# Order of VectorE's work in the attention of the second block, and where the heads' norm weight is multiplied in

## The reference, cut to what matters

```python
ya = sparse_attention(aq, ak, av, iq, ik, iw, k_sel)      # 8 heads of 64, keys chosen by an index (top 128)
yb = diff_attention(bq, bk, bv, lam)                      # 4 heads, two softmaxes each, values of 128
#   p = softmax(q k / 8, causal);  attn = p[:, :, 0] - lam * p[:, :, 1];  yb = attn @ v
yb = (rms_norm(yb, b_subln) * (1.0 - lam_init))           # b_subln: one weight for each of the 128 columns of a head
g_a, g_b = split(sigmoid(gates + gate_bias))
merged = g_a * (ya @ w_up_a) + g_b * (yb @ w_up_b)
x = x + merged @ w_out
```

## Time and profile before

| | |
|---|---|
| time, median of 3 runs | 2447.8 us (2446.33 to 2454.46) |
| the profiled execution | 2451.56 us, span 2450.0 us |
| PE busy | 2279.2 us (93%) |
| DVE, ACT, POOL busy | 1266.3 us (52%), 838.8 us (34%), 363.2 us (15%) |
| mean granted clock of TensorE | 0.976 |

### The profile page before, as it was taken

The page is one execution under the profiler, slowest core; times in us unless marked ns, Lnnn a source line. Parts: engine busy times, 40 slices in busy tenths (PEclk is TensorE's granted clock), DMA queues, the critical chain, the costliest instruction groups (busy, mean ns, idle before and its releaser), DMA issues.

```text
span 2450.0 us, 28572 instructions
## 1 busy us (share of the span) xinstructions
PE 2279.2 (93%) x11029; PEld 1718.7 (70%) x11029; DVE 1266.3 (52%) x2310; ACT 838.8 (34%) x1478; POOL 363.2 (15%) x273
## 2 busy tenths in 40 slices
PE   7899988789889999899999999999989999999999
PEld 4785676455334776677778888887667778888887
DVE  4633446631113696676554434458776746443442
ACT  4334433321101445444242223244454334322221
POOL 0111123000000454331000000035433200000000
PEclk9999999889999999999999999999999999999999
DMA  8116310269998121221223222222212212333222
GB/s 294 53 53 208 110 35 10 95 235 334 359 383 289 61 80 59 61 69 52 78 86 101 97 95 95 91 78 77 78 53 69 69 43 95 97 100 96 91 90 78
DMA packets 198570, 281.61 MB, mean 115 GB/s; under 512 B 13308, under 2 KB 125732, under 8 KB 198436
## 3 DMA queue, kind: packets, MB, share of 16 engines
q1 hardware_dynamic: 197872, 278.60, 34.1%
q10 hardware_dynamic: 564, 1.18, 0.1%
HBM read 277.65 MB, written 2.10 MB: 114 GB/s over the span
## 4 chain that ended last, share of the span: by engine, by line
PE 72%; DVE 15%; DMA 5%; ACT 5%; issue 2%; SPq 1%; POOL 0%; DVEq 0%; ACTq 0%
PE PS L621 19%; PE PS L623 18%; PE PS L622 18%; PE PS L2248 3%; PE PS L1378 3%; PE PS L2288 2%; DMA RX<-in_w_up_dram 1%; DVE AL L824 1%; PE PS L2179 1%; PE PS L1360 1%; DVE AL L816 1%; DMA RAW<-in_w_up_dram 1%; DVE AL L803 1%; PE PS L2304 1%; DVE CO L800 1%
## 5 line engine op out<-in xcount | busy, mean ns | idle before, releaser
L621 PE MATMUL PS<-OPH,WHI 128*128 128x512 f32 x1224 | 503.2, 411 | 15.5 <-DVE OPL L1414 7.7
L623 PE MATMUL PS<-OPH,WLO 128*128 128x512 f32 x1224 | 486.5, 397 | 0.0
L622 PE MATMUL PS<-OPL,WHI 128*128 128x512 f32 x1224 | 482.2, 394 | 0.0
L609 POOL TENSOR_TENSOR WLO<-RAW,WHI 128x1024 fp32r<-128x1024 f32 (+1 forms) x107 | 253.0, 2370 | 1310.5 <-ACT WHI L576 1307.2
L576 ACT ACTIVATE WHI<-RAW 128x1024 fp32r<-128x1024 f32 (+2 forms) x286 | 294.1, 1032 | 445.7 <-PE PS L623 437.0
L593 DVE TENSOR_TENSOR WLO<-RAW,WHI 128x1024 fp32r<-128x1024 f32 x179 | 214.6, 1200 | 382.8 <-ACT WHI L576 382.8
L621 PEld LDWEIGHTS PS<-OPH,WHI 128*128 128x128 f32 x1224 | 233.1, 190 | 81.9 <-issue 32.0
L623 PEld LDWEIGHTS PS<-OPH,WLO 128*128 128x128 f32 x1224 | 232.7, 190 | 53.1
L622 PEld LDWEIGHTS PS<-OPL,WHI 128*128 128x128 f32 x1224 | 233.7, 191 | 46.5 <-issue 1.0
L621 PE MATMUL PS<-WHI,OPH 128*128 128x512 f32 (+2 forms) x576 | 235.3, 409 | 8.2 <-ACT AL L758 3.6
L623 PE MATMUL PS<-WHI,OPL 128*128 128x512 f32 (+2 forms) x576 | 221.3, 384 | 0.0
(11 more groups left out here) (410 smaller groups left out, 3316.0 us busy)
## 6 DMA issues: line engine op xcount, KB each, us to landing
RAW<-in_w_in_dram SPq DMA_DIRECT2D x102, 512.0 KB, 3.5
RAW<-in_w_ffn_in_dram SPq DMA_DIRECT2D x88, 512.0 KB, 3.5
RX<-in_w_gate_dram SPq DMA_DIRECT2D x42, 512.0 KB, 7.6
RX<-in_w_down_dram SPq DMA_DIRECT2D x42, 512.0 KB, 11.4
RAW<-in_w_ffn_out_dram SPq DMA_DIRECT2D x40, 512.0 KB, 3.4
RAW<-in_w_mod_dram SPq DMA_DIRECT2D x36, 512.0 KB, 4.5
RX<-in_w_up_dram SPq DMA_DIRECT2D x32, 512.0 KB, 11.3
RAW<-in_w_up_dram SPq DMA_DIRECT2D x25, 512.0 KB, 9.8
```

The lines of the kernel that those rows point to most:

```text
L609: lo_p.up(G.e.tensor_tensor(q.flo, q.flat, q.fhi.bitcast(F32), ALU.subtract), ("w", q.i))
L621: T.e.matmul(o, a[0], b[0], start=first, stop=False)
L622: T.e.matmul(o, a[0], b[1], start=False, stop=False)
L623: return T.e.matmul(o, a[1], b[0], start=False, stop=last)
```

## The change

It does six things, in both layers. (1) DVE's dense pieces of a step come ahead of its index entries, and `best_at` takes one entry in step 0 and none in steps 9 and 14 (38 in all in place of 39). (2) A row's end is done by itself, at lag 7, in place of two at lag 4. (3) The leasts of kind a are taken in pairs, at even steps. (4) From step 49 a step has one dense piece; PE does one more behind the last values, turns the last block, and does the last two then; ACT and DVE split that block ahead of what remains of their dense pieces. (5) The multiplication by `b_subln` goes: it is loaded as a column into `VT`, and becomes the scale of ACT's copy and DVE's subtraction behind the transposes; the multiplication by the reciprocal root is done for one block each in steps 21, 23, 25 and 27. (6) L3077, one element per partition, is a tensor_scalar with two scalar operands.

```diff
-                          ("gb", d["gate_bias_2"].rearrange("a (k p) -> (a k) p", p=128))))):
+                          ("gb", d["gate_bias_2"].rearrange("a (k p) -> (a k) p", p=128)),
+                          ("sub", d["b_subln_2"])))):
...
-                          ("bq", "b_q_norm_2", 64), ("bk", "b_k_norm_2", 64), ("sub", "b_subln_2", 128))] +
+                          ("bq", "b_q_norm_2", 64), ("bk", "b_k_norm_2", 64))] +
...
+            V.e.tensor_copy(VT[:, 192:194], ps(PB["vt"])[:, 192:194])
...
-        def act_block_split(name, dst):
+        def act_block_split(name, dst, gain=None):
             A.wait_ge(*turned["blk", name])
-            split_a.up(A.e.activation(dst, ps(PB["blk", name]).rearrange("p (g n) -> p g n", g=4), ACT.Copy), name)
-
-        def dve_block_split(name, low, high):
+            split_a.up(A.e.activation(dst, ps(PB["blk", name]).rearrange("p (g n) -> p g n", g=4), ACT.Copy,
+                                      scale=1.0 if gain is None else gain), name)
+
+        def dve_block_split(name, low, high, gain=None):
...
+                split_v.up(V.e.scalar_tensor_tensor(low, src, gain, high.bitcast(F32), ALU.mult, ALU.subtract), name)
...
-                at = each_third(y, 4)
-                if at and at[1] % 2:
-                    for r in (first + 4 * at[0] + at[1] - 1, first + 4 * at[0] + at[1]):
-                        dve_rope_end(r)
+                at = each_third(y, 7)
+                if at:
+                    dve_rope_end(first + 4 * at[0] + at[1])
...
-        parts_at = lambda s: 3 if s < 32 else 2
+        parts_at = lambda s: 3 if s < 32 else 2 if s < 49 else 1
...
-        best_at = lambda s: 1 if s in (1, 2, 3, 9, 14, 15) else 2 - s % 2 if 18 <= s < 32 else 2 if 32 <= s < 38 else 0
+        best_at = lambda s: 1 if s in (0, 1, 2, 3, 15) else 2 - s % 2 if 18 <= s < 32 else 2 if 32 <= s < 38 else 0
...
-                some(dense, 1)
+                some(dense, min(parts_at(s) - 1, 1))
...
+            some(dense, 1)
+            pe_block_turned(("a2", l, 7), YR2[:, 3], tidy["a2", l, 7], D)
             for _ in dense:
                 pass
-            pe_block_turned(("a2", l, 7), YR2[:, 3], tidy["a2", l, 7], D)
...
-                    for v in u.cs:
+                    for v in u.cs if u.kind == "b" else [] if u.h % 2 else units[s:s + 2]:
...
-                    t = diff_v.up(V.e.scalar_tensor_tensor(u.r, u.cs[0].rs, LAM[:, 4 * l:4 * l + 1], u.r, ALU.mult, ALU.mult))
+                    t = diff_v.up(V.e.tensor_scalar(u.r, u.cs[0].rs, LAM[:, 4 * l:4 * l + 1], u.r, ALU.mult, ALU.mult))
...
-                    if u.no in (15, 16):
-                        for i in (0, 1) if u.no == 15 else (2, 3):
-                            y = QB[:, :, 128 * i:128 * i + 128]
-                            V.wait_ge(*diff_v.up(V.e.tensor_tensor(
-                                y, y, Y16[:, i].unsqueeze(2).to_broadcast([128, 4, 128]), ALU.mult)))
-                            diff_v.up(V.e.tensor_tensor(y, y, R(f"sub{l}").unsqueeze(1).to_broadcast([128, 4, 128]),
-                                                        ALU.mult), ("y", l, i))
+                    if u.no in (16, 18, 20, 22):
+                        i = (u.no - 16) // 2
+                        y = QB[:, :, 128 * i:128 * i + 128]
+                        diff_v.up(V.e.tensor_tensor(y, y, Y16[:, i].unsqueeze(2).to_broadcast([128, 4, 128]), ALU.mult), ("y", l, i))
+                some(dense, parts_at(s))
                 some(index_, best_at(s))
-                some(dense, parts_at(s))
+            dve_block_split(("a2", l, 7), OPL[:, 0:4, sparse_tokens(7)], OPH[:, 0:4, sparse_tokens(7)])
             for _ in dense:
                 pass
-            dve_block_split(("a2", l, 7), OPL[:, 0:4, sparse_tokens(7)], OPH[:, 0:4, sparse_tokens(7)])
```

More of the change, by code:

```diff
@@ L1406, in pe_block_turned @@
             ring.give(b, (split_v, name))
-        def act_block_split(name, dst):
+        def act_block_split(name, dst, gain=None):
             A.wait_ge(*turned["blk", name])
-            split_a.up(A.e.activation(dst, ps(PB["blk", name]).rearrange("p (g n) -> p g n", g=4), ACT.Copy), name)
-        def dve_block_split(name, low, high):
+            split_a.up(A.e.activation(dst, ps(PB["blk", name]).rearrange("p (g n) -> p g n", g=4), ACT.Copy,
+                                      scale=1.0 if gain is None else gain), name)
+        def dve_block_split(name, low, high, gain=None):
             V.wait_ge(*split_a[name])
-            split_v.up(V.e.tensor_tensor(low, ps(PB["blk", name]).rearrange("p (g n) -> p g n", g=4), high.bitcast(F32),
-                                         ALU.subtract), name)
+            src = ps(PB["blk", name]).rearrange("p (g n) -> p g n", g=4)
+            if gain is None:
+                split_v.up(V.e.tensor_tensor(low, src, high.bitcast(F32), ALU.subtract), name)
+            else:
+                split_v.up(V.e.scalar_tensor_tensor(low, src, gain, high.bitcast(F32), ALU.mult, ALU.subtract), name)
         def pe_mod_rest():
@@ L2872, in act_between @@
                     for i in (0, 1) if y == TURN0 + 1 else (2, 3):
-                        act_block_split(("b2", l, i), OPH[:, 4:8, 128 * i:128 * i + 128])
+                        act_block_split(("b2", l, i), OPH[:, 4:8, 128 * i:128 * i + 128], vc("sub", l))
                 if y in (TURN0 + 6, TURN0 + 7):
@@ L2902, in dve_between @@
                         c = slice(128 * i, 128 * i + 128)
-                        dve_block_split(("b2", l, i), OPL[:, 4:8, c], OPH[:, 4:8, c])
+                        dve_block_split(("b2", l, i), OPL[:, 4:8, c], OPH[:, 4:8, c], vc("sub", l))
                 if y in (TURN0 + 6, TURN0 + 7):
@@ L3169, in act_att2 @@
                 some(dense, parts_at(s))
+            act_block_split(("a2", l, 7), OPH[:, 0:4, sparse_tokens(7)])
             for _ in dense:
                 pass
-            act_block_split(("a2", l, 7), OPH[:, 0:4, sparse_tokens(7)])
         SQ4 = MQ[:, :].rearrange("p (i n) -> p i n", i=2)
```

## The result

The changed kernel takes 2422.86 us (median of 4 runs, 2421.6 to 2423.34), the kernel before 2447.48 us beside it (4 runs). The ratio is 0.9884 with a 95% interval of 0.9866 to 0.9902 (the quotient of the two medians, 0.9899, lies inside it). By the medians that is a gain of 24.6 us: inside the range, 12 us short of the forecast of 2411. The profiled execution fell from 2451.56 to 2422.81 us and its span from 2450.0 to 2421.0.

A forecast was written before the change was run, and what follows sets the result against it. PE bounds the kernel, with at most 57 us of attention waits and slow clock to gain. Layers of 22.1 and 21.3 us, minus 0.6 and a 6 us reserve, gave 37 us: 2447.8 to 2411, likeliest 2398 to 2424, range to 2432.

The forecast's parts named there:

- What bounds the kernel: PE, busy 93% of the span; up to 38.2 us of attention waits and 18.7 us of slow clock, 57 us together.
- Ends by themselves, steps 6 to 9: Waits of 4.57 us fall to 2.5, a new one of about 1.5 us in step 8; gain 3.0 us in layer 1.
- Steps 11 to 14: Waits for leasts behind paired ends at L846 go, none replaces them; gain 4.5 us in layer 1, 3.7 in layer 0.
- the sum: Layer 1 22.1 us and layer 0 21.3, minus 0.6, is 42.8; 6 us taken off gives a gain of 37 us.
- Index behind dense pieces, step 15: The 2.60 us wait for L2896 loses the index entry ahead of it; 1.3 us stays, gain 1.3 us.
- Leasts by pairs, and the heads' norm: Step 22's 2.53 us wait and a slow stretch go, 4.2 us; steps 38 and 42 give 4.4 us.
- The end: PE's waits of 0.86 and 2.36 us at the attention's end go, with 1.5 us of clock: 4.7 us a layer.
- The reserve: 6 us taken off for one further wait of 1.3 us with its slow stretch per layer, as DVE becomes tighter.
- DVE as the bound: Rival: waits come back as others in steps 32 to 37; gain about 18 us, 2430; chance 0.23 together with the clock rival.
- The clock did come back: Rival held that slow stretches stay at other small waits: 22 us, 2426; chance 0.23 together with DVE as the bound.
- The slower rival: Ends at lag 7 finish too late for PE's turns at lag 9; 2455 if pairs also hold up copies; chance 0.04.
- The tensor_scalar: L3077 in the step 7 chain may pass GpSimd; booked at nothing, bounds nothing and 2 us at two or three places a layer.

The follow-up runs named there:

- the best kernel: Changed kernel with GpSimd's low parts of two weights ahead of rows 2 and 3, and step 15's dense pieces ahead of the block's output: 2405.75 us, ratio 0.9817.
- the kernel with ends in pairs: Changed kernel with two rows' ends together at lag 4 again, as in the kernel before: 2408.96 us, ratio 0.9829.

## Why the prediction was right in sign and 12 us short

**What bounds the kernel** held. In each of the thirteen kernels I took the time ahead of layer 0's step 0, the waits and the clock off the span. What is left lies between 1485.7 and 1490.0 us, while the spans run from 2402.5 to 2450.0. So the time of this kernel is its waits and its clock in the two attentions, and the gain could not exceed the 57 us of the prediction; the best kernel got 44.

**Ends by themselves, steps 6 to 9: this step failed.** I expected 1.0 us left at the first wait (0.75 came) and a new one of 1.5 us in step 8. It is 4.78 us, and not for a least but for GpSimd's low part. Waits of 4.57 us became 5.53, and the slow stretch, twice as long but half of it inside the wait, cost its 1.7 us as before: a loss of 1.0 us in layer 1 where 3.0 of gain stood. I followed the end that moved on DVE and asked what stands behind it there. I did not ask who waits for it: GpSimd's fourth row does, and low parts stand behind that.

**Steps 11 to 14: this step failed too,** with the words "no wait should replace it". The leasts' 2.92 us went as said and 4.10 us came, with a slow stretch as before: a loss of 1.2 us in place of a gain of 4.5. Both places and both layers together had 14.2 us in the sum. By the trace they lost 7.4 us (waits and clock gave back 24.0 us in all, and the other places below make 31.4 of it), and by the kernel with ends in pairs 14 us relative to leaving them alone. It is the same omission in both places, since k's rows stand on GpSimd as q's do.

**Index behind dense pieces, step 15:** 1.3 us left, 1.29 measured, and alone 2.8 us for 2.6. The size came from reading the start of L2564 and of L2896.

**Leasts by pairs, and the heads' norm:** the sizes held, with 2.53 us and a slow stretch at step 22 gone, and 3.48 us and a slow stretch at steps 38 and 42, of which 0.52 came back ahead of L3051. The reasons were half right. I said that the pair frees step 22; the runs show that it is freed without the pair, and point to the lighter norm.

**The end:** 4.7 us a layer in the sum. 3.22 us of waits and one stretch, 4.9 us, are gone in the change, and alone it measured 4.0 a layer. No wait stands ahead of L1405 or of the product with w_up_a.

**The reserve and the clock.** The 6 us for a further wait of DVE and the 0.6 us for ScalarE's column scale were not needed: behind step 15 the only wait left is the 0.52 us. And the clock gave back more than I had booked. The kernel with ends in pairs loses 3.4 us to it in both attentions, before 18.2: 14.8 us, where the sum had 9 to 10 for these parts. That is why the forecast of 2411 nearly holds for a kernel without the ends by themselves (2409.0), though it was made with 14.2 us for them: the errors had opposite signs.

**The rivals.** The time lies between the forecast and "DVE as the bound", but neither is what happened. DVE was no bound: PE's new waits end on GpSimd, and of the leasts only those of steps 7 and, in layer 0, 11 are still waited for, 0.75 and 0.47 us in the trace. The clock did come back wherever the waits were gone. The slower rival, ends that meet their transposes, didn't come: inside the attention L847 waits 0.47 us in layer 0 for a least and nowhere for its row. It had the right edit for the wrong reader of it.

**The tensor_scalar** was booked at nothing, and the difference of 1.6 us between the two forms is within their runs. The Trainium skill ("SBUF — State Buffer", "Who interferes with whom") says that a VectorE instruction with two SBUF inputs contends with a GpSimd one that reads SBUF, the first to issue holding the ports until it is done, and that tensor_scalar can be locked out in the same way through its two-port mode. The first half agrees with 2.87 us for L804 and 2.0 us for the old form. The second did not occur with one element per partition: all 32 took 272 to 276 ns, one of them at 1761.59 in the middle of GpSimd's subtractions. It saved PE nothing. L3085 behind it reads two inputs and takes most of the blocked time over: the two took 2.48 us together at 1825.94 (L3085 2.17 of them), and 2.79 us in the old form at 1827.73 (L3083 2.00 of them). At no place of the attention is the pair more than 0.7 us shorter in the new form, and PE's waits are the same with both.

## What to carry to other kernels

When an instruction is moved, list its readers on all engines, not only its neighbours on its own, and for each reader what stands behind it in that queue; here the price was on an engine that is busy for 15% of the span. Where a consumer takes work in a batch (four rows in one go), its producers may come in pairs for a reason, and splitting them needs the batch split too. Count waits together with the clock behind them, and price them for the kernel in which they will stand: the same two waits of 4 to 5 us in a layer cost 4.4 us where the places had slow stretches anyway, and 13.9 us where half of these had gone.

## What the runs showed of the hardware

- A slow stretch of TensorE's clock (1.2 in place of 2.4 GHz) was either 3.41 or 6.83 us long in the attentions: all eleven of before 3.41, but 6.83 behind twelve of the sixteen waits of 4 to 5 us in the four kernels that have them, and in others behind a few waits of 2.4 to 3.4 us and one of 1.2 us. Up to 3.6 us of a long one fell into the wait itself, where it costs nothing. It did not follow from one wait alone: the kernel with ends in pairs has the same waits in steps 7 to 11 of both layers (2.13 and 1.22, then 1.89 us in layer 0; 2.12, 1.23 and 1.90 in layer 1), with two slow stretches in layer 0 and none in layer 1. What made the difference I did not settle. I take it as the main reason why sums made place by place missed by some us in either direction.
- VectorE's product of 128 x 512 with two SBUF inputs (L804) took 0.69 us alone, 1.24 us when it began 2.0 us into GpSimd's subtraction of 2.73 us, and 2.87 us when it began with one. Each of the two long ones ended 0.5 to 0.6 us after the subtraction did.
- One element per partition takes 0.05 us longer as tensor_scalar with two scalar operands (273 ns) than as scalar_tensor_tensor (221 ns), but none of 32 was held up by GpSimd, where the other takes up to 2.1 us.
